# An expert-weight stream in a hybrid decoder step: weights asked for from the last attention scores on, two more places in the later 64-row blocks, and a combining step over eight PSUM banks

## The reference, cut to what matters

```python
logits = (xt @ w_router + b_router)          # 264 tokens, 8 experts
top_val, top_idx = lax.top_k(logits, 2)
gate = jax.nn.softmax(top_val, axis=-1)
...
swiglu(xb, w_gate[e], w_up[e], w_down[e])    # 1024 -> 2816 -> 1024, rows grouped by expert
...
y = x + sum over the two experts of gate * row
return rmsnorm(y, norm_final)
```

## Time and profile before

| what | value |
|---|---|
| runs of the kernel before | 1195.99 us (median of 3; 1194.99 to 1199.93) |
| the profiled execution's own time | 1192.92 us |
| its span, first to last instruction | 1191.3 us |
| mean granted TensorE clock | 0.988 of 2.4 GHz |
| PE / DVE / ACT / POOL busy | 95% / 67% / 58% / 4% of the span |
| HBM read, written | 366.93 MB, 26.27 MB |
| unit loads | 264, of 1,024 KB |

### The profile page before, as it was taken

The page is one execution under the profiler, slowest core; times in us unless marked ns, Lnnn a source line. Parts: engine busy times, 40 slices in busy tenths (PEclk is TensorE's granted clock), DMA queues, the critical chain, the costliest instruction groups (busy, mean ns, idle before and its releaser), DMA issues.

```text
span 1191.3 us, 21103 instructions
## 1 busy us (share of the span) xinstructions
PE 1130.0 (95%) x7944; PEld 929.5 (78%) x7944; DVE 798.7 (67%) x1266; ACT 693.7 (58%) x1082; POOL 53.5 (4%) x79
## 2 busy tenths in 40 slices
PE   6999999999999898966999999998999999999987
PEld 6989999999996678844888888655887887887544
DVE  6677666665652986512998997205998998997214
ACT  5665444554546678402887886105887887886011
POOL 1000000000430000100000000000000000000200
PEclk9999999999999899996999999999999999999999
DMA  9575545454666984999999999999999999998993
GB/s 346 188 250 202 173 182 195 160 211 170 257 198 207 378 281 177 418 419 418 420 418 420 405 420 417 369 419 419 419 419 419 420 421 394 396 419 327 392 409 132
DMA packets 69271, 390.28 MB, mean 328 GB/s; under 512 B 6742, under 2 KB 25818, under 8 KB 30714
## 3 DMA queue, kind: packets, MB, share of 16 engines
q1 hardware_dynamic: 64138, 367.45, 77.8%
q0 software_dynamic: 5040, 21.58, 5.0%
HBM read 366.93 MB, written 26.27 MB: 330 GB/s over the span
## 4 chain that ended last, share of the span: by engine, by line
PE 79%; DMA 7%; DVE 7%; ACT 4%; issue 2%; SPq 0%; DVEq 0%; ACTq 0%
PE bank L2326 12%; PE bank L2328 12%; PE bank L2327 12%; PE bank L1781 9%; PE bank L1782 9%; PE bank L1783 9%; DMA raw<-in_moe 6%; PE bank L2277 5%; PE bank L2260 2%; PE bank L2232 1%; ACT arena L875 1%; DMA ring<-in_wd 1%; PE bank L2311 1%; DVE d_lo L1173 1%; DVE w_lo L1606 1%
## 5 line engine op out<-in xcount | busy, mean ns | idle before, releaser
L1606 DVE TENSOR_TENSOR w_lo<-raw,w_hi 128x1024 fp32r<-128x1024 f32 x330 | 392.8, 1223 | 31.3 <-ACT w_hi L993 20.6
L993 ACT CAST w_hi<-raw 128x1024 fp32r<-128x1024 f32 x330 | 339.4, 1054 | 75.4 <-PE bank L2328 47.6
L1173 DVE TENSOR_TENSOR d_lo<-ring,d_hi 128x1024 fp32r<-128x1024 f32 x120 | 147.8, 1237 | 84.8 <-ACT d_hi L746 82.5
L1781 PE MATMUL bank<-hA_hi,d_hi 128*128 128x264 f32 x640 | 184.5, 288 | 12.3 <-DVE hA_lo L1163 9.8
L1782 PE MATMUL bank<-hA_lo,d_hi 128*128 128x264 f32 x640 | 182.6, 285 | 0.0
L1783 PE MATMUL bank<-hA_hi,d_lo 128*128 128x264 f32 x640 | 182.3, 285 | 0.0
L2326 PE MATMUL bank<-w_hi,xg_hi 128*128 128x512 f32 x440 | 172.7, 393 | 7.5 <-DVE w_lo L1606 7.5
L2328 PE MATMUL bank<-w_hi,xg_lo 128*128 128x512 f32 x440 | 171.9, 391 | 0.0
L2327 PE MATMUL bank<-w_lo,xg_hi 128*128 128x512 f32 x440 | 171.8, 390 | 0.0
L746 ACT CAST d_hi<-ring 128x1024 fp32r<-128x1024 f32 x120 | 125.0, 1045 | 77.8 <-PE bank L1783 68.6
L1781 PEld LDWEIGHTS bank<-hA_hi,d_hi 128*128 128x128 f32 x640 | 121.6, 190 | 14.7 <-issue 12.7
(11 more groups left out here) (386 smaller groups left out, 1651.8 us busy)
## 6 DMA issues: line engine op xcount, KB each, us to landing
raw<-in_moe SPq DMA_DIRECT2D x258, 1024.0 KB, 17.9
ring<-in_wd SPq DMA_DIRECT2D x29, 2048.0 KB, 8.2
out_rows<-zeros SPq DMA_DIRECT2D x1, 6656.0 KB
slot_rows<-zeros SPq DMA_DIRECT2D x1, 6144.0 KB
early_units<-in_moe SPq DMA_DIRECT2D x6, 1024.0 KB, 11.5
xs<-slot_rows POOLq DMA_DIRECT2D x5, 512.0 KB, 8.3
out_rows<-yrow POOLq DMA_DIRECT2D x5, 512.0 KB, 8.0
arena<-in_cmp_pages POOLq DMA_DIRECT2D x16, 128.0 KB, 3.3
```

The lines of the kernel that those rows point to most:

```text
L993: nc.scalar.copy(w_hi[:, i % NSPLIT, :], raw[:, raw_slot(u), ITEM * (i % 2):ITEM * (i % 2) + ITEM])\
L1173: V.tensor_tensor(d_lo[:, n % NDS, :], raw_item(n), d_hi[:, n % NDS, :].bitcast(F32), ALU.subtract)\
L1606: V.tensor_tensor(w_lo[:, i % NSPLIT, :], raw[:, raw_slot(i // 2), ITEM * (i % 2):ITEM * (i % 2) + ITEM], w_hi[:, i % NSPLIT, :].bitcast(F ...
L1781: T.matmul(out, w_hi_[:, j, :], hi[:, k, :], start=(first and j == 0), stop=False)
```

## The change

It does four things. (1) SP waits for `so_ready` and `kv_stored` and the last score product (`s_done`) and then issues eight units (0 to 5, 10 and 11), before the wait on `o_done`; units 6 to 9 follow that wait, unit 12 follows the moment when the ring slot of the output projection's first tile has been split, 13 and 14 the end of the projection, 15 and 16 its sum. Some small tiles of the attention (`vtp`, `gtok`, `vcp`) and the squares of the fourth norm move in SBUF so that the places are free by then. (2) In both small blocks units 0 and 1 go to two places outside the ring (`hB` and `htok`, `NSPARE` = 2); the ring then holds the units from 2 on. POOL's gather into these tiles waits for unit 1 of the last block to have been used. (3) The copies of the last block's rows are made in halves, and the eight products go to eight different banks. (4) Each chunk's squares go to PE for the mean at once, eight times three matmuls; DVE's sums in pairs and the `stay_awake` matmuls at the end are gone, and root and reciprocal are one instruction each.

```diff
+EARLY_PLACE = [3, 5, 0, 1, 2, 4]
+SCORED, PARAMS_PLACE = 6, NRAW - 1
+NSPARE = 2
-        LAST_BANKS = [T0, T1, B[0], B[1], STAT, T0, T1, B[0]]
+        LAST_BANKS = [T0, T1, B[0], B[1], B[3], STAT, MISC, B[2]]
+        squared = [sqr[:, k, :] for k in range(KC)]
+        squared3 = [slc_v[:, a:a + NT] for a in [NT * k for k in range(5)] + [2 * KC * NT - NT * k for k in (3, 2, 1)]]
...
+        def kept(t, kind):
+            if isinstance(t, int):
+                return NEXTRA + NSPARE * sum(k == "small" for k, _, _ in WALK[:t + 1])
+            return NEXTRA + NSPARE * ((kind == "small") + sum(k == "small" for k, _, _ in WALK))
+        def raw_slot(t, kind, u):
+            return u if kind == "tiny" and u < NRAW else (u - kept(t, kind)) % NRAW
+        def spared(kind, u):
+            return kind == "small" and u < NSPARE
+        def unit_at(t, kind, u):
+            if kept_early(kind, u):
+                return early_units[:, EARLY_PLACE[u - NRAW], :]
+            if spared(kind, u):
+                return (hB[:].rearrange("p k t -> p (k t)"), htok[:].rearrange("p t n -> p (t n)"))[u][:, 0:UNIT]
+            return raw[:, raw_slot(t, kind, u), :]
...
-            sp.wait_ge(o_done, NH)
             sp.wait_ge(so_ready, 1)
             sp.wait_ge(kv_stored, 16)
-            for u in range(NRAW):
-                sp.dma_start(raw[:, u, :], moe[0, u]).then_inc(raw_in[u], 16)
+            sp.wait_ge(s_done, NH)
+            for u in range(SCORED):
+                first_unit(u)
+            first_unit(PARAMS_PLACE)
+            first_unit(NRAW)
+            sp.wait_ge(o_done, NH)
+            for u in range(SCORED, PARAMS_PLACE):
+                first_unit(u)
+            sp.wait_ge(*used["bo0"])
+            first_unit(NRAW + 1)
             projected(sp, "bo", 7)
+            first_unit(NRAW + 2)
+            first_unit(NRAW + 3)
             sp.wait_ge(sum_step, 28)
-            for u in range(NRAW, NRAW + NEXTRA):
-                sp.dma_start(early_units[:, u - NRAW, :], moe[0, u]).then_inc(early_in[u - NRAW], 16)
+            first_unit(NRAW + 4)
+            first_unit(NRAW + 5)
...
+            def small_units(e, t, i, j):
+                for u in range(UNITS):
+                    if NSPARE <= u < NSPARE + NRAW:
+                        after_wide(j, u - NSPARE + UNITS - NRAW)
+                    elif u >= NSPARE + NRAW:
+                        after_small(i, u - NRAW)
+                    load(e, t, "small", u)
...
+            pool.wait_ge(small_used, LAST * UNITS + NSPARE)
             for t in range(3):
                 for m in range(2):
                     nc.gpsimd.indirect_dma_start(back[t][m][0:rows_of(t), :], None, out_rows, index(1, t, m)).then_inc(back_in, 16)
...
-            nc.scalar.copy(yrow[0:64, 0:512], B[2][0:64, :]).then_inc(left_ready, 1)
+            for half in range(2):
+                nc.scalar.copy(yrow[0:64, 256 * half:256 * half + 256], B[2][0:64, 256 * half:256 * half + 256]).then_inc(left_ready, 1)
...
-            nc.scalar.activation(tok_rstd[:, 0:2], B[2][:, 0:2], ACT.Sqrt, bias=vector("eps")[:, 0:1])
-            nc.scalar.activation(tok_rstd[0:NS, 2:3], B[2][0:NS, 2:3], ACT.Sqrt, bias=vector("eps")[0:NS, 0:1]).then_inc(tok_std, 1)
+            nc.scalar.activation(tok_rstd[:, 0:3], T0[:, 0:3], ACT.Sqrt, bias=vector("eps")[:, 0:1]).then_inc(tok_std, 1)
...
-            for c in range(KC):
-                add_combined(1, c)
-                if c in (2, 4, 6, 7):
-                    j = c // 2 - 1 if c < 7 else 3
-                    dve.wait_ge(sq_ready, 32 + 2 * j + 2)
-                    V.tensor_tensor(sq_last[:, 2 * j, :], sq_last[:, 2 * j, :], sq_last[:, 2 * j + 1, :], ALU.add).then_inc(sum_step, 1)
+            for n in range(KC):
+                add_combined(1, n)
...
-            def last_mean(j):
-                stay_awake(B[3], 4 if j == 3 else 1)
-                pe.wait_ge(sum_step, 28 + j + 1)
+            def last_mean(n):
+                pe.wait_ge(sq_ready, 32 + n + 1)
                 for t, (a, z) in enumerate(spans):
-                    i = T.matmul(B[2][0:z - a, t:t + 1], sq_last[:, 2 * j, a:z], mean[:, 0:1], start=(j == 0 and t == 0), stop=(j == 3 and t == 2),
+                    i = T.matmul(T0[0:z - a, t:t + 1], sq_last[:, n, a:z], mean[:, 0:1], start=(n == 0 and t == 0), stop=(n == KC - 1 and t == 2),
...
-            for c in range(KC):
-                combine(c)
-                if c >= 5:
-                    last_mean(c - 5)
-            last_mean(3)
-            stay_awake(B[3], 3)
-            pe.wait_ge(tok_scale, 4)
+            for n in range(KC):
+                combine(n)
+            for n in range(KC):
+                last_mean(n)
+            pe.wait_ge(tok_scale, 3)
```

More of the change, by code:

```diff
@@ L580, in _ @@
                 after_small(LAST - 1, u + UNITS - NRAW)
-                load(e, u)
+                load(e, len(WALK), "wide", u)
             with sp.Fori(NWIDE, wides) as w:
@@ L585, in _ @@
                     after_wide(w, u - NRAW)
-                    load(e, u)
+                    load(e, w + WIDE_STEP, "wide", u)
                 e = expert_of(bass.ds(w + NSMALL + 1, 1))
@@ L589, in _ @@
                     after_wide(w, u + UNITS - NRAW)
-                    load(e, u)
+                    load(e, w + (WIDE_STEP + 1), "wide", u)
             e = expert_of(bass.ds(wides + NSMALL, 1))
@@ L593, in _ @@
                 after_wide(wides, u - NRAW)
-                load(e, u)
+                load(e, wides + WIDE_STEP, "wide", u)
             e = expert_of(slice(LAST, LAST + 1))
[L596 to L601, removed]
+            small_units(e, wides + (WIDE_STEP + 1), LAST, wides)
             for q in range(4):
@@ L1245, in _, with add_chunk @@
                         .then_inc(gated_lo, 1)
-            def add_chunk(c, norm, stage, item, squared=sqr, rests=()):
+            def add_chunk(c, norm, stage, item, squares=squared, rests=()):
                 rest_to(stage, item - 1)
@@ L1254, in add_chunk @@
                     rest_weighted(vector(r[0]), c, *r[1:])
[L1255 removed]
+                add_up(squares, c, sq_ready, 8 * norm + c + 1)
                 rest_to(stage, item)
@@ L1726, in _ @@
                 if next_kind(t) == "wide":
-                    first_items(sum(k == "wide" for k, _, _ in WALK[:t + 1]))
+                    first_items(t + 1, sum(k == "wide" for k, _, _ in WALK[:t + 1]))
             dve.wait_ge(blk_ready, 1)
@@ L2209, in down @@
                     pe.wait_ge(hmT_lo, t * FT + f + 1)
-                    wait_landed(pe, t, u)
-                    weights = unit_at(t, u)
+                    wait_landed(pe, t, "tiny", 0, u)
+                    weights = unit_at(t, "tiny", u)
                     for j in range(2):
@@ L2255, in down @@
                     pe.wait_ge(hmT_lo, t * FT + f + 1)
-                    wait_landed(pe, t, u)
-                    weights = unit_at(t, u)
+                    wait_landed(pe, t, "small", s, u)
+                    weights = unit_at(t, "small", u)
                     for j in range(2):
```

121 lines of the change are left out of this document (61 added, 60 removed).

## The result

| what | before | after |
|---|---|---|
| median of the runs (lowest to highest) | 1197.11 us (1194.99 to 1199.93, n = 4) | 1187.24 us (1186.97 to 1189.8, n = 4) |
| ratio of the times | | 0.9911, 95% interval 0.9883 to 0.9939 |
| profiled execution, and its span | 1192.92, 1191.3 us | 1189.8, 1188.2 us |
| mean granted clock in it | 0.988 | 0.983 |

The kernel is 9.9 us faster, 0.89%. 1182.5 was predicted; 1187.24 lies within the range given, 1177 to 1190, and 0.2 us outside the likeliest case's own range, 1179 to 1187. The two profiled executions are only 3.1 us apart: the one of before is the fastest of all executions of before, the one of after the slowest of these four. So a comparison of spans says little here, and the comparison has to go stage by stage.

What follows compares the result with a forecast made beforehand. Two limits alternate, PE and a DMA stream of 264 units at 2.5 us each. Terms 5.0 + 2.4 + 2.9 + 3.2 = 13.5 us take the median from 1195.99 to 1182.5 us, range 1177 to 1190.

Steps and rivals of the forecast that it cites:

- The early loads: Attention's end to first wide block: first unit lands 19.7 us earlier, 5.0 us of it kept, bounds 3.8 to 6.4.
- the two gaps: Before the tiny block: DMA share near 0 from 478 until 490 us, and a dip just before 504.
- Rival (a): Attention's end and tiny block: the early loads give nothing that lasts, about 0.5 us, time 1187; chance 0.10.
- The first spares: First small block: two units asked for earlier fill idle DMA time, 2.4 us gained, bounds 1.0 and 2.4.
- I expect no new gap: First small block: unit 13 still waits for the block's third unit, behind the row stores, so 2.4 us remain.
- The last spares: Last small block: two units asked for earlier make its last DMA step 2.9 us earlier, bounds 1.6 and 4.5.
- The end: Last row copies to the spread: mean 2.9 us earlier, root and reciprocal 0.3, together 3.2; bounds 2.4 and 3.9.
- ACT sets the pace, not DVE, PE or a bank: Mean in the end: ACT's squares come 0.34 us apart, eight of them done at 1179.65 us.
- the last three matmuls for the mean add 0.6: Mean in the end: after the last square only 0.6 us of PE work, done at 1180.3 instead of 1183.24.
- rival (c): End: gains nothing, since PE waits between chunks without filling matmuls and its clock falls; 1185.7 us, chance 0.04.
- Rival (b): Early loads: the whole lead shows, 19.7 us instead of 5.0, time 1168; chance 0.02.
- rival (d): First wide block: slower kernel if PE's clock stays at the lower level, 41 us of it needed; chance 0.04.

Runs made afterwards that it cites:

- e6: After with four units instead of eight issued at the last scores, the other four after `o_done`: 1188.7 us, ratio 0.9905 to before.
- e2: After with `NSPARE` = 0, no places outside the ring for the small blocks: 1192.02 us, ratio 0.9940 to before.
- e8: After with DVE's pair sums behind the eight additions and eight filling matmuls ahead of the first mean matmul: 1186.86 us, ratio 0.9920 to before.
- e7: Before with the new end alone, late loads and no spare places: 1196.47 us, ratio 0.9979 to before.
- e3: After with the first loads late again, as in before: 1191.78 us, ratio 0.9947 to before.
- after again: The same program as after, timed and profiled once more: 1186.68 us, ratio 0.9918 to before.
- e4: After with DVE's pair sums put behind the eight additions, halving PE's products for the mean: 1187.14 us, ratio 0.9896 to before.
- e5: After with a wide mean: 128x128 weights stationary, squares moving, no spreading matmuls, root and reciprocal on 128x264: 1185.57 us, ratio 0.9883 to before.

## Why the prediction was right, and where it was wrong

The early loads and the last block's spare places did what the prediction said, for 6.7 of the 7.9 us that it gave them. Of its four terms three came out within their own bounds and the end's, 1.8 by the stages for 2.4 to 3.9, did not: the end gained less, and not by the pace that the prediction named. All four came out below the value taken, so that the total lies near the far end of the stated range.

**The early loads: right in mechanism, 4.2 us instead of 5.0.** The restart points, the unit counts and the two gaps are where the prediction put them, all 3.9 us later with the attention's end. 4.2 lies near the lower bound, 3.8, which was the count with none of the slot-row writes helped. The rows of POOL's first such write, shown above, say why: it starts with unit 17's issue, at 505.12 and 505.23 in after as at 501.23 and 501.34 in before, so the writes came when the gap was over, not into it. That e6 loses nothing confirms the sum's structure: two restarts eat the lead, not the start. Rival (a), early loads that give nothing, was priced at 1187, which is the time measured; its mechanism did not take place. A time that fits is no evidence for the rival that named it.

The first two early units landed after these times in the trace of after (issue to landing, us):

```profile
DMA to landing us min/median/max: 4.8/5.8/6.9
```

The first is 0.5 us less than the 5.3 that the sum used for a restart. The fixed part is 4.8 - 2.5 = 2.3 us, nearer to the 2.0 us that the Trainium skill, DMA: Bandwidth & Descriptors, section Anatomy of one DMA, gives for the GpSimd path than the 2.8 of before was; unit 17, issued with the slot-row writes, still took 5.8. So the two figures of a restart lie on both sides of the 5.3.

**The first spares: 1.1 instead of 2.4 us.** The share over these 20 us rose from 0.89 to 0.99, 2.0 us of transfers, yet only 1.1 reached the block's end. So the step that took the filled idle time for the gain, and "I expect no new gap", were wrong. The windows split the 20 us and go on behind them; over 745 to 755 the share rose from 0.80 to 1.01, and over the next ten it fell, after and below it before:

```profile
755.00:765.00 10.00, 10.00 (x82) 5.67 (x80) 1.26 (x5) 0.59 (x3) 0.55 (x1) 1.00 0.96 372
```

```profile
755.00:765.00 10.00, 10.00 (x82) 5.63 (x80) 1.27 (x5) 0.83 (x3) 0.55 (x1) 1.00 1.02 397
```

That is 0.6 us of new idle time. Besides, the wide block's row store, which used to pass in the idle stretch, now lands 8.0 us after its issue instead of 3.6, and the fetch of the next rows starts at 761.09 instead of 757.12, so that it takes the queue's time in the block. How much of the rest that is, no run separates. The kernels with early loads and no spares (e2, 68.2) stand behind before (67.5 to 68.0) here, which points to some of the early lead being given back, but 0.2 to 0.7 us in single profiles can't carry that.

**The last spares: 2.5 instead of 2.9 us,** inside the bounds; the whole block is shorter by it, and its last DMA step ends at 1137.11 + 22.00 = 1159.11, 58.1 us from the block's first product against 1162.48 - 1102.15 = 60.3. POOL's added wait cost nothing: its first gather stands at 1107.72 now, 6.7 us behind the block's first product, where before it stood 9.7 behind.

**The end: the failed step is "ACT sets the pace, not DVE, PE or a bank", and "the last three matmuls for the mean add 0.6".** Squares come 2.59 / 8 = 0.32 us apart, as said, and are done at 1173.35 + 2.59 = 1175.94. But the mean's 48 records take 5.76 us, and PE's weight loads for them 5.67: 6 x 0.12 = 0.72 us a chunk, over twice the time of a square. PE ends 3.6 us after the last square. The earlier trace rows held a price that would have said so: x6 in 0.47 us is one such group of three products (its first weights load while the filling matmuls ahead of it still run), and 8 x 0.47 = 3.8 us is already more than the 2.7 us of eight squares at 0.34. The prediction charged one group, 0.6 us, for the last chunk alone.

That error was met by another of opposite sign. The old end was priced from one execution in which the clock stayed up (12.3 us), whereas three others show 14.4, 15.8 and 16.0, with the filling matmuls on the path at the lower clock. The new end was never seen with the full clock to its last step: in all six profiles the clock fell before the first scaled output. In after:

```profile
1178.60:1181.90 3.30, 2.71 (x12) 2.28 (x12) 0.18 (x1) 0.26 (x1) 0.00 (x0) 0.50 0.01 2
```

The spread took 1.76 us there and 0.91 in before's first profile. So 12.5 against 12.3 isn't like against like. Where the clock fell at about the same moment (the table under e8), the new end takes 12.5 against 14.4 and 13.6 and 13.8 against 15.8 and 16.0: 1.9 to 2.2 us less. Over all, the mean of four profiles with the old end is 14.6 and of the six with the new one 12.9, 1.8 us less; e7's runs say 2.5; 3.2 was predicted. At the full clock the gain would be less: e3, where the clock fell last, takes 12.1, and with a spread of 0.91 instead of 1.76 it would take about 11.3, by estimate 1 us less than before's 12.3. So the gain is not the one that the prediction counted, an earlier end of the mean paced by ACT. That it is larger at the lower clock fits the filling matmuls, 4.3 us of the old path there, being gone; but no run took them alone out of the old end, so this share isn't shown.

Of rival (c), the clock falling because PE waits between the chunks, the fall came about and the reason didn't: PE has no gap in the 5.76 us of the mean, and the clock fell with the filling matmuls too, in three of four.

**The sum.** 4.2 + 1.1 + 2.5 + 1.8 = 9.6 us, against 9.9 (after) and 11.4 (after again) between the medians. The 3.9 us that lack to the 13.5 are 0.8, 1.3, 0.4 and 1.4, term by term. Rival (b) had nothing for it, and rival (d) neither: wide 1 and 2 take 190.0 us against 190.1. The lower clock at the start of a wide block that makes 191.3 or 286.0 of these stages comes and goes in executions of before as of changed kernels. On rival (d) the prediction cited the Trainium skill, TensorE: Matmul & The Clock Gate, section HAM oscillation; the trace agrees as to the place, with a clock of 0.90 over 505 to 555, and it is no more pronounced than the 0.88 of before.

## What to carry to other kernels

A lead in a stream of transfers is kept only as far as there are places for it: find every later restart that the places or another event set, and count the lead there, not where it begins; e6 shows that half of the early loads did all the work. When a step is handed from one engine to another (here sums from DVE to PE), multiply its own row's price by its new count and compare with the pace of the neighbour before saying who sets it. And price the stage you replace from more than one execution if the clock takes part in it; work that is there only to keep the clock up is on the path at the lower clock when it fails.

## What the runs showed of the hardware

- The same program's clock differs between executions: at the same point of the attention 0.52 and 1.00, and the same end takes 12.3 to 16.0 us. Executions with low stretches near 405 and 434 us take up to 5.0 us longer from the same point of the attention to the experts. The time goes with it: before's profiles of 1192.92, 1198.09 and 1201.83 us have mean clocks of 0.988, 0.981 and 0.974.
- An fp32 product of one column, with fresh 128x128 weights, costs 0.11 us a record at the full clock, of which there are two for each product (e3, 48 in 5.36 us; e8, 24 in 2.71), 0.12 in after, whose last microsecond is at the lower level, and 0.17 in e4, nearly all at the lower level. One of 264 columns, its weights loaded too, costs 0.24 a record (e5, full clock). The one column costs about half as much as 264.
- A DVE reciprocal took 0.18 us for 128x3 (after) and 1.80 for 128x264 (e5); the additions of 128x264 took 2.81 / 8 = 0.35 each (after).
- Filling matmuls didn't hold the clock: with them in place it fell 7.0, 7.2 and 9.2 us after the last down product's start in three of four executions. What sets the moment is open.
